# First weight tile's products between the norms, and the memory output projection by token chunk with the router beside it

## The reference, cut to what matters

```
def memory_block(x, mk, mv, norm_mem_q, w_mem_q, w_mem_o):
    q = (rmsnorm(x, norm_mem_q) @ w_mem_q).reshape(bsz, L, MEM_HEADS, MEM_HEAD_DIM)
    s = einsum('bqhd,bkhd->bhqk', q, mk) * (MEM_HEAD_DIM ** -0.5)
    o = einsum('bhqk,bkhd->bqhd', softmax(s), mv).reshape(bsz, L, D_MODEL)
    return x + o @ w_mem_o                      # D_MODEL = 1024

def hier_moe(x, norm_ffn, w_group_router, w_expert_router, w_gate_e, w_up_e, w_down_e):
    h = rmsnorm(x, norm_ffn)
    p_sel, g_sel = top_k(softmax(h @ w_group_router), 1)         # 1 of 4 groups
    le = (h @ w_expert_router).reshape(-1, 4, 4)                 # 4 experts a group
    le_sel = take_along_axis(le, g_sel)
    top_v, top_i = top_k(le_sel, 2)
    gate = softmax(top_v) * p_sel
    for e in range(16):
        he = silu(h @ w_gate_e[e]) * (h @ w_up_e[e])             # width 512
        out = out + dense_w[:, e:e + 1] * (he @ w_down_e[e])
    return x + out
```

## Time and profile before

| | us |
|---|---|
| median of three runs | 1349.79 |
| profiled execution, its own time | 1356.14 |
| its span | 1354.4 |
| TensorE matmul busy | 1206.1 (89%) |
| TensorE weight load busy | 1069.2 (79%) |
| VectorE busy | 701.1 (52%) |
| ScalarE busy | 563.4 (42%) |
| GpSimd busy | 113.8 (8%) |
| HBM read, written | 178.41 MB, 18.65 MB |

### The profile page before, as it was taken

How to read it: one execution, slowest core, us unless ns; L and a number is a source line. 1 busy time by engine, 2 the same in 40 slices (tenths; PEclk the granted TensorE clock), 3 DMA queues, 4 the chain that set the end, 5 groups by cost and what they waited for, 6 DMA issues and landing times.

```text
span 1354.4 us, 18178 instructions
## 1 busy us (share of the span) xinstructions
PE 1206.1 (89%) x7830; PEld 1069.2 (79%) x7830; DVE 701.1 (52%) x777; ACT 563.4 (42%) x687; POOL 113.8 (8%) x172
## 2 busy tenths in 40 slices
PE   4998999999989699999999898889739999999960
PEld 3996668999967499999899897579728788888850
DVE  6213543663268462323424613522578988888845
ACT  5214452333246342222215423412136777777732
POOL 2000211000035200000000000000010000000003
PEclk8998989999968899999999999989559999999985
DMA  8331000232300023232426512000559999999926
GB/s 277 101 109 62 1 0 15 64 94 60 87 11 2 31 55 86 78 86 86 157 70 214 191 63 78 1 1 1 194 203 353 383 407 399 403 395 388 360 86 203
DMA packets 95317, 198.30 MB, mean 146 GB/s; under 512 B 4280, under 2 KB 71984, under 8 KB 82944
## 3 DMA queue, kind: packets, MB, share of 16 engines
q1 hardware_dynamic: 86672, 167.52, 35.2%
q0 software_dynamic: 6256, 21.16, 4.4%
q10 hardware_dynamic: 2304, 8.39, 1.5%
HBM read 178.41 MB, written 18.65 MB: 145 GB/s over the span
## 4 chain that ended last, share of the span: by engine, by line
PE 69%; DVE 13%; ACT 9%; issue 4%; DMA 3%; POOL 1%; ACTq 0%; POOLq 0%; DVEq 0%
PE ps L1688 44%; PE ps L770 5%; DVE buf_r L712 4%; ACT buf_r L705 4%; PE ps L1776 3%; PE ps L780 2%; PE ps L1876 2%; PE ps L2006 1%; ACT buf_r L404 1%; PE ps L1754 1%; PE ps L1790 1%; DVE buf_r L862 1%; DMA buf<-y_rows,buf 1%; PE ps L642 1%; DVE buf_r L408 1%
## 5 line engine op out<-in xcount | busy, mean ns | idle before, releaser
L1688 PE MATMUL ps<-buf_r,buf_r 128*128 128x288 f32 (+1 forms) x4752 | 611.1, 291 | 8.4 <-DVE buf_r L408 7.0
L1688 PEld LDWEIGHTS ps<-buf_r,buf_r 128*128 128x128 f32 x4752 | 608.3, 189 | 9.6 <-DVE buf_r L408 7.6
L398 DVE TENSOR_TENSOR buf_r<-buf,buf_r 128x2048 fp32r<-128x2048 f32 (+2 forms) x53 | 117.6, 2219 | 245.3 <-ACT buf_r L392 245.3
L712 DVE TENSOR_TENSOR buf_r<-buf,buf_r 128x2048 fp32r<-128x2048 f32 x96 | 213.9, 2285 | 0.0
L770 PE MATMUL ps<-buf_r,buf_r 128*128 128x512 f32 x768 | 186.6, 398 | 2.4 <-DVE buf_r L862 2.4
L705 ACT CAST buf_r<-buf 128x2048 fp32r<-128x2048 f32 x96 | 178.0, 1908 | 0.0
L770 PEld LDWEIGHTS ps<-buf_r,buf_r 128*128 128x128 f32 x768 | 143.2, 190 | 33.6 <-DVE buf_r L862 3.3
L392 ACT CAST buf_r<-buf 128x2048 fp32r<-128x2048 f32 (+2 forms) x53 | 96.6, 1823 | 150.2 <-PE ps L1688 150.2
L780 PE MATMUL ps<-buf_r,buf_r 128*128 128x512 f32 x384 | 93.1, 399 | 1.4 <-DVE buf_r L881 1.4
L780 PEld LDWEIGHTS ps<-buf_r,buf_r 128*128 128x128 f32 x384 | 73.2, 191 | 18.6 <-DVE buf_r L881 1.6
L404 ACT CAST buf_r<-ps 128x1024 fp32r<-128x1024 f32 (+1 forms) x32 | 25.6, 801 | 85.0 <-PE ps L754 60.5
(11 more groups left out here) (274 smaller groups left out, 1104.6 us busy)
## 6 DMA issues: line engine op xcount, KB each, us to landing
buf<-in_w_gate_e SPq DMA_DIRECT2D x32, 1024.0 KB, 8.4
buf<-in_w_up_e SPq DMA_DIRECT2D x32, 1024.0 KB, 7.5
buf<-in_w_down_e SPq DMA_DIRECT2D x32, 1024.0 KB, 7.4
buf<-in_w_in SPq DMA_DIRECT2D x16, 1024.0 KB, 5.6
buf<-in_w_in SPq DMA_DIRECT2D x17, 512.0 KB, 5.3
buf<-in_w_mem_kv SPq DMA_DIRECT2D x8, 1024.0 KB, 5.8
y_rows<-buf ACTq DMA_DIRECT2D x16, 512.0 KB, 9.0
buf<-in_x_prompt SPq DMA_DIRECT2D x8, 512.0 KB, 4.8
```

The source lines that it names most:

```text
L398: nc.vector.tensor_tensor(r32(raw), raw, w_hi(n), ALU.subtract).then_inc(wl_ready, 1)
L712: nc.vector.tensor_tensor(e_lo(t), e_raw(t), e_hi(t), ALU.subtract).then_inc(wl_ready, 1)
L1688: last = nc.tensor.matmul(out, a, b, start=(k == 0 and j == 0), stop=(k == len(parts) - 1 and j == 2))
```

## The change

The computation stays the same. Four places change.

Start: seven small loads (gains and convolution weights) move from GpSimd's queue to ScalarE's, ahead of the table load; GpSimd makes the constants first and issues its six other loads after them. TensorE turns three chunks, then makes the first tile's products with the turns of chunks 3 and 4 between them; the memory input's two turns go ahead of product 10.

```diff
+            turn(0)
+            pe.wait_ge(vec_loaded, 16 * 7)
+            nc.tensor.transpose(bank(7)[:, 0:100], VEC[0:100, :], IDENT[0:100, 0:100]).then_inc(vec_psum, 1)
+            turn(1)
+            turn(2)
+            pe.wait_ge(wr_loaded, 96)
...
             for i in range(20):
                 t, m = divmod(i, 5)
+                if i in (1, 2):
+                    turn(i + 2)
+                if i == 2:
+                    pe.wait_ge(vec_ready, 2)
+                if i == 10:
+                    turn(5)
+                    turn(6)
```

```diff
             for i in range(4 * NC_):
-                t, m = divmod(i, NC_)
+                m, t = divmod(i, 4)
                 if m == 0:
                     pe.wait_ge(wl_ready, W_MO + t + 1)
-                if i >= 4:
-                    pe.wait_ge(x2_ready, i - 3)
-                rproj(i % 4, W_MO + t, m, OTH_F, OT_F).then_inc(mo_psum, 1)
-            for i, (_, n) in enumerate(CH):
-                norm_turn(pe, N_I + i, XNR[:n, i, :], n, 4)
-                if i:
-                    router_scores(pe, i - 1)
+                if i >= 3:
+                    pe.wait_ge(x2_ready, i - 2)
+                rproj(i % 3, W_MO + t, m, OTH_F, OT_F).then_inc(mo_psum, 1)
+                if m and t == 1:
+                    n = CH[m - 1][1]
+                    norm_turn(pe, N_I + m - 1, XNR[:n, m - 1, :], n, 4)
+                if m and t == 3:
+                    router_scores(pe, m - 1)
...
+                if a in (8, 13):
+                    split_high(act, W_MO + 2 + (a > 8))
```

```diff
+            one_hot(dve, 0, GM[0])
+            dve.wait_ge(g_psum, 1)
+            row_index(dve, 0, 1)
+            one_hot(dve, 1, GM[1])
+            one_hot(dve, 2, GM[2])
+            dve.wait_ge(g_psum, 2)
+            row_index(dve, 1, 3)
...
             sp.wait_ge(mo_psum, 4 * NC_)
-            sp.wait_ge(hn_stored, 16 * NC_)
-            sp.wait_ge(ht_ready, N_I + NC_)
             for t in range(NT):
+                if t == 6:
+                    sp.wait_ge(ht_ready, N_I + NC_)
+                    sp.wait_ge(xg_loaded[0], 16)
```

```diff
+        GROUPS = ((3, 6), (6, 9), (9, 12), (12, 14), (14, 16))
...
+                if e == 0:
+                    route_gates(pe)
                 pe.wait_ge(he_ready, e + 1)
...
+                if e < len(GROUPS):
+                    route_group(pe, e)
...
                 expert_low(dve, t - 1)
                 expert_low(dve, t)
+                if 1 <= e <= len(GROUPS):
+                    group_out(dve, e - 1)
                 dve.wait_ge(sg_ready, e + 1)
...
+                if e == 0:
+                    dve.wait_ge(g_psum, 3)
+                    gates_out(dve, 0, 3)
+                if e < len(GROUPS):
+                    group_one_hots(dve, e)
                 for i in range(1, 5):
                     expert_low(dve, t + i)
-                if e == 1:
-                    rows_step()
+                if e == len(GROUPS) + 1:
+                    rows_step(dve)
...
+                for g, (e0, _) in enumerate(GROUPS):
+                    if e == e0:
+                        pool.wait_ge(idx_ready, 4 + 2 * g)
```

More of the change, by code:

```diff
@@ L169, in encoder_step @@
         MT = A.view(KD, ML)
+        spot = A.mark()
+        A.back(base)
+        HI_MO = [A.view(WT)]
+        A.back(spot - KD * ML)
+        HI_MO.append(A.view(WT))
         YSBT = A.view(4, T)
@@ L291, in encoder_step @@
         NF = A.view(D)
-        GM = [A.half(NC_, P) for _ in range(2)]
+        GM = [A.half(NC_, P) for _ in range(3)]
         POSB = A.half(NC_, NE)
@@ L630, in route_dve @@
-            return rows_step
-        route_steps = {}
+            dve.wait_ge(pos_psum, 1)
+            pos = bank(7)[:, 128:208].rearrange("p (c e) -> p c e", c=NC_)
+            go(dve, v.scalar_tensor_tensor(out=POSM, in0=pos, scalar=1.0, in1=MK, op0=ALU.add, op1=ALU.mult))
+            go(dve, v.tensor_scalar(POSB, POSM, -1.0, float(P), ALU.add, ALU.min))
+            assert route_count[0] == route_slots
+            one_hot(dve, 0, GM[0])
+            dve.wait_ge(g_psum, 1)
+            row_index(dve, 0, 1)
@@ L643, in router_scores, with slot_rows @@
                                         start=(k == 0), stop=(k == KD - 1))
+            last.then_inc(lg_psum, 1)
+        def slot_rows(pe, e, buf, c0, c1):
+            for c in range(NC_):
+                last = nc.tensor.matmul(bank(7)[:, 5 * e + c0:5 * e + c1], buf[0:CH[c][1], c, :],
+                                        TW[0:CH[c][1], c, e, c0:c1], start=(c == 0), stop=(c == NC_ - 1))
             return last
         def route_pe(pe):
-            router_scores(pe, NC_ - 1).then_inc(lg_psum, 1)
@@ L648, in route_pe @@
[L648 removed]
+            router_scores(pe, NC_ - 1)
+            pe.wait_ge(route, route_mask)
             for c in range(NC_ + 1):
                 for c2 in range(min(c + 1, NC_)):
[L651 to L652 removed]
+                    n = CH[c2][1]
+                    last = nc.tensor.matmul(bank(7)[:, 128 + 16 * c:144 + 16 * c], (TSTR_B if c2 == c else ONES_B)[0:n, :],
+                                            MK[0:n, c2, :], start=(c2 == 0), stop=(c2 == min(c, NC_ - 1)))
@@ L653, in route_pe @@
             last.then_inc(pos_psum, 1)
-            for e in range(NE):
-                pe.wait_ge(g_ready, e + 1)
-                for c in range(NC_):
-                    last = nc.tensor.matmul(bank(2)[:, 5 * e:5 * e + 5], GM[e % 2][:, c, :], TW[:, c, e, :],
-                                            start=(c == 0), stop=(c == NC_ - 1))
-                last.then_inc(g_psum, 1)
-            pe.wait_ge(idx_ready, 2)
+            pe.wait_ge(g_ready, 1)
+            slot_rows(pe, 0, GM[0], 0, 2).then_inc(g_psum, 1)
@@ new lines, in route_pe, with route_gates, route_group @@
+            pe.wait_ge(g_ready, 3)
+            slot_rows(pe, 1, GM[1], 0, 2)
+            slot_rows(pe, 2, GM[2], 0, 2).then_inc(g_psum, 1)
+            pe.wait_ge(idx_ready, 2)
+        def route_gates(pe):
+            pe.wait_ge(route, route_steps["gates"])
+            for e in range(3):
+                last = slot_rows(pe, e, GM[e], 2, 5)
+            last.then_inc(g_psum, 1)
+        GROUPS = ((3, 6), (6, 9), (9, 12), (12, 14), (14, 16))
+        def route_group(pe, g):
+            for e in range(*GROUPS[g]):
+                pe.wait_ge(g_ready, e + 1)
+                last = slot_rows(pe, e, GM[e % 3], 0, 5)
+            last.then_inc(g_psum, 1)
@@ L934, in overflow_pe @@
             for c in range(NC_):
-                last = pe.matmul(bank(7)[:, 0:5], GM[0][:, c, :], TWO[:, c, :], start=(c == 0), stop=(c == NC_ - 1))
+                n = CH[c][1]
+                last = pe.matmul(bank(7)[:, 0:5], GM[0][0:n, c, :], TWO[0:n, c, :], start=(c == 0), stop=(c == NC_ - 1))
             last.then_inc(g_psum, 1)
```

397 lines of the change are left out of this document (223 added, 174 removed).

## The result

The changed kernel took 1339.42 us (median of four, 1334.55 to 1341.26) against 1351.86 for the kernel before, ratio 0.9893 with a 95% interval of 0.9845 to 0.9941. The ratio is not that of the medians, which lie 12.4 us apart; it says 14.5 us less, between 8 and 21. A later comparison (six executions, 1343.92, against eleven, 1352.91) gave 0.9935, 0.9912 to 0.9957: 8.8 us less. The prediction was -16.1, to 1333.7, range 1326 to 1342. Direction and mechanism came out as forecast; the traces make the sum of the touched stages -17.6, and the timed executions give less.

The account below looks back on a forecast made before the run. TensorE, busy for 89% of the span, was taken as the bound, with only idle or slow stretches to win. Terms -6.6 + 1.9 - 22.5 + 11.1 = -16.1 us, taking the median from 1349.79 to 1333.7, range 1326 to 1342.

Parts of the forecast that it names:

- Start, -6.6 forecast: Kernel start: fifth product copied 8.7 us earlier, less 2.1 for the memory input's turns; -6.6 us.
- The memory turns' +2.1: Kernel start: the memory input's two turns now stand inside a busy TensorE, costing 2.1 us.
- Attention, +1.9: Memory attention: two ScalarE casts after steps 8 and 13 each make the chain 0.95 us late; +1.9 us.
- Projection to first turn, -23.3: Projection to first expert: gather issued 25.7 us earlier, its landing 2.4 slower; gates' matmuls not included.
- the gates' 0.8: Before the hidden turn: 15 gate matmuls stand ahead of it on TensorE, costing 0.8 us.
- round-robin rule: First gather: DMA engines alternate between queues packet by packet, so it shares with tiles and lands in 7.5 us.
- Experts, +11.1: Expert loop: one-hots, index and gate steps lengthen passes 0 to 5, and `rows_step` grows; +11.1 us.
- part 3: Projection to first expert: turns and router products among the products, earlier gather, slower landing, gate matmuls; -22.5 us.
- A: Expert loop: VectorE's idle time absorbs the router, only about 3 us added; total -24, 1325.7 us; chance 0.12.
- B: DMA queues: late gathers and late tiles 6 and 7 give some 8 us back; total -8, 1341.8; chance 0.17.
- C: Projection: turns and narrow router products lower TensorE's clock, four times 5.5 us; total +6, 1356; chance 0.04.
- D: Start: gives nothing, as loads on two queues delay tile and gains alike; total -9.5, 1340.3; chance 0.07.

Follow-up runs that it names:

- the undoing: Changed kernel with its start alone put back as before (constants on GpSimd's queue, all seven turns first); ratio 0.9958 to the kernel before.
- the tile first: Changed kernel with ScalarE's and VectorE's start order mended and the first weight tile issued ahead of three chunks of rows; ratio 0.9895 to the kernel before.
- second trace after: The changed kernel, unaltered, profiled a second time; first memory score stretch 722.0 us, second to last turn of expert rows 268.3 us.

## Why the prediction was right or wrong

- **Start, -6.6 forecast.** -3.3 in the traces (means of two and of eight), -5.0 by the undoing. The order of events was right, two sizes were not: the tile landed after 12.9 us in place of 11.4, and the first product took 4.62 (5.41 to 5.46 in five of the eight traces) where I had 2.89. That product followed 4.77 us of idleness. A granted clock of 0.53 over it is seen only with the tile first, where it took 5.32; in the other traces with the new start the record reads 1.00, so the clock as the cause is likely but not shown. The wait for the bank was right in size, 0.95 for 0.7. ScalarE stood idle from 11.0 to 16.25, and from 12.6 on chunk 0's high part could have been made there; I had put it behind the tile without asking. The memory turns' +2.1 was right (1.91).
- **Attention, +1.9.** The mechanism was right: each cast delayed the chain, by 0.74 where I had 0.95, and TensorE's idle time grew by 1.5 us. The stage's length, +1.2 in the first pair of traces and -1.6 in the second, does not show it, since the clock moves TensorE's busy time in this stage by 3 us and more, 46.7 to 52.2 us over the traces.
- **Projection to first turn, -23.3 (the gates' 0.8 apart).** -24.4 and -24.0. Last product 66.7 us after the start (67.6 forecast), logits +7.6 (7.5), gather out +15.9 (15), landing 7.5 (8.5). Router products 1.85, turns 1.04. This part carries the result. The round-robin rule of the Trainium skill (DMA: Bandwidth & Descriptors, Queues, rings and completion order), by which I had worked out 7.5 as an estimate, came nearer than my 8.5. That is partly luck: it started from the 6.1 of a gather alone, and two later traces show 4.5 and 4.7 with the tiles mostly landed, so the six tiles cost nearer 3 us than the 1.4 of that estimate. The second trace after has 7.9.
- **Experts, +11.1.** The 0.8 of the gates' matmuls stands in my sum twice, here in pass 0 and in the -22.5 of part 3; without that the forecast is -16.9. Measured: +11.0 and +8.9 from second to last turn, but not by the terms. Pass 0 cost 2.87 for 1.7: TensorE's two sets of slot matmuls (0.95 and 0.96, on its path) and a wait of 0.71 for a low part added up, where I took the longer of both. Passes 1 to 5 cost 1.63, 1.64, 0.80, 0.94 and 0.35, together 5.4 for 8.85. The five small steps in front took 0.75 (1057.51 to 1058.26), where I had 1.05, and I had taken TensorE's own 1.2 and 0.6 for the part behind; VectorE's rule alone gives 0.75 + 2.2 - 1.24 = 1.7 and 0.75 + 1.47 - 1.24 = 1.0, near what was measured. The row steps cost 2.5 more than before for 0.6: 0.95 of length and 1.5 of clock. The 1.5 of clock is in the first trace alone, which is most of the difference to +8.9. The errors cancelled, and the agreement to 0.1 us is luck.
- **Rivals.** A: pass times and the one-hots put first exclude it. B: the gather landed sooner than forecast, and TensorE's turns waited for a gather only once. C: granted clock 1.00 through the projection; turns 1.04, router products 1.85. Its rule in the Trainium skill (TensorE: Matmul & The Clock Gate, PE-mode transpose) had no effect to be seen among products. D: the start undone was slower.
- **What stays open.** By two traces of each kernel the touched stages differ by 17.6 us, by timed executions the whole by 9 to 14.5. Falls of the clock outside the change are of that size. The mean clock that each timed execution was granted goes the same way: the kernel before ranges from 1345.45 us at 0.939 to 1359.63 at 0.928, the changed one from 1334.55 at 0.949 to 1348.03 at 0.940. In which stages the unprofiled executions lost it, I can't say.

## What to carry to other kernels

Joining the projection with the norms, turns and router products behind it was worth 7 us. The one-hot matrices and gates, taken from ahead of the first gather into the expert loop, made the second turn of rows 21 us earlier and cost 10 us in longer passes. The wider steps from logits to mask gave 3 us (4.7 in place of 8.0). In a loop that one engine nearly fills, price added work on that engine in full in front of the product that others wait for, and by its length less the engine's visible wait behind it, and look whether the other engine's share adds up with it. Where TensorE paces a stage, split the stage's length into TensorE's busy and idle time before you explain a difference: here the idle time repeated to 0.2 us and showed what an edit did, while the busy time moved with the granted clock, by more than the edit was worth.

## What the runs showed of the hardware

In pass 7 two executions of one kernel show the same waits, yet the clock fell in one only; after, then after again:

```profile
1132.42 3.08 PE L823 MATMUL ps<-buf_r,buf_r 128*128 128x512 f32 x12 [0.94 <-DVE buf_r L924]
1137.43 0.83 PE L807 MATMUL ps<-buf,buf 128*128 128x128 f32 x4 [1.92 <-DVE buf L945]
1137.93 4.60 PE L823 MATMUL ps<-buf_r,buf_r 128*128 128x512 f32 x12
```
```profile
1143.02 3.08 PE L823 MATMUL ps<-buf_r,buf_r 128*128 128x512 f32 x12 [0.98 <-DVE buf_r L924]
1148.02 0.75 PE L807 MATMUL ps<-buf,buf 128*128 128x128 f32 x4 [1.92 <-DVE buf L945]
1148.53 3.02 PE L823 MATMUL ps<-buf_r,buf_r 128*128 128x512 f32 x12
```

Of ten traces with the row steps in that place seven read 22.96 to 22.99 us for the pass and three 21.44 or 21.45. The granted clock over these stretches:

```profile
1137.00:1142.00 5.00, 4.57 (x15) 3.75 (x16) 3.45 (x4) 2.38 (x2) 0.00 (x0) 0.66 0.80 331
```
```profile
1148.00:1153.00 5.00, 4.98 (x24) 4.16 (x24) 3.58 (x3) 3.82 (x4) 0.00 (x0) 1.00 0.78 283
```

A gather of 0.5 MB took 4.5 us with four weight tiles issued some 10 us ahead of it, 4.7 with six issued 16 us ahead, 7.5 and 7.9 with six issued 10 us ahead. The first weighted product after the norms took from 4.62 to 5.46 us in eight executions with the same start, where the next ones took 3.1; the granted clock over it was recorded as 1.00 in all eight.
